# Two weight tiles at once in each output projection, and modulation vectors from one-column products

## The reference, cut to what matters

```python
mod = silu(c) @ ada_w[layer] + ada_b[layer]        # (3 * D,): shift, scale, gate
h = rms_norm(x, norm_w[layer]) * (1 + scale) + shift
y = mixer(h @ w_in)                                # layer's own mixer, its gate path with SiLU
x = x + gate * (y @ w_out)                         # w_out: 1024 x 1024
# after the last layer: out = rms_norm(x, final_norm_w)
```

## Time and profile before

| | us |
|---|---|
| median of 3 runs | 3574.63 |
| lowest, highest | 3570.79, 3578.21 |
| profiled execution, whole | 3582.37 |
| its span, first to last instruction | 3580.6 |
| TensorE busy in it | 3331.5 |

### The profile page before, as it was taken

One profiled execution on the slowest core, in us unless ns is written; L12 is line 12 of the kernel. 1 busy time (PEld: TensorE's weight loads), 2 busy tenths in 40 slices (PEclk: granted clock), 3 DMA queues, 4 the chain that ended last, 5 costly groups with the idle time before them and its releaser, 6 DMA issues.

```text
span 3580.6 us, 49279 instructions
## 1 busy us (share of the span) xinstructions
PE 3331.5 (93%) x18911; PEld 2689.9 (75%) x18911; DVE 2303.9 (64%) x3820; ACT 1509.9 (42%) x2635; POOL 943.0 (26%) x487
## 2 busy tenths in 40 slices
PE   5998899799999999999989999988998999999998
PEld 3776678677887777888767777876778777788877
DVE  6887888763466774565557766996536554556554
ACT  4665365333344124322466655653334431342234
POOL 1003233211233124222510043432121422422233
PEclk9999899899999999999989999998999999999999
DMA  4434455434753532111231123554449221221112
GB/s 170 131 111 129 126 145 147 124 105 127 251 179 89 166 93 88 50 37 36 65 129 55 46 72 84 159 139 111 126 112 349 74 59 53 60 72 40 32 48 100
DMA packets 569015, 383.83 MB, mean 107 GB/s; under 512 B 67802, under 2 KB 522445, under 8 KB 568781
## 3 DMA queue, kind: packets, MB, share of 16 engines
q1 hardware_dynamic: 568781, 380.68, 35.6%
HBM read 299.01 MB, written 80.54 MB: 106 GB/s over the span
## 4 chain that ended last, share of the span: by engine, by line
PE 71%; DVE 16%; DMA 4%; ACT 4%; issue 4%; SPq 1%; POOL 1%; ACTq 0%; DVEq 0%; POOLq 0%
PE bank L230 55%; DVE dnp_conv L1837 3%; DVE dnp_diag_term L1915 2%; DVE h_lo L700 1%; PE bank L2359 1%; DVE res_ada_sums L279 1%; DVE dnp_diag_inv L1918 1%; PE bank L2562 1%; DVE res_h L688 1%; DMA dn_planes<-dnp_inv_t 1%; PE bank L2589 1%; POOL w_lo L212 1%; PE bank L1527 1%; DVE res_sq_total L727 1%; PE bank L2603 1%
## 5 line engine op out<-in xcount | busy, mean ns | idle before, releaser
L230 PE MATMUL bank<-h_hi,w_hi 128*128 128x512 f32 x3616 | 1478.9, 409 | 49.6 <-DVE h_lo L126 16.0
L230 PE MATMUL bank<-h_hi,w_lo 128*128 128x512 f32 x3616 | 1428.0, 395 | 0.0
L230 PE MATMUL bank<-h_lo,w_hi 128*128 128x512 f32 x3616 | 1427.6, 395 | 0.0
L212 POOL TENSOR_TENSOR w_lo<-w_raw,w_hi 128x1024 fp32r<-128x1024 f32 x262 | 648.2, 2475 | 1447.8 <-ACT w_hi L203 1447.8
L230 PEld LDWEIGHTS bank<-h_hi,w_hi 128*128 128x128 f32 x3616 | 691.1, 191 | 227.4 <-issue 57.1
L230 PEld LDWEIGHTS bank<-h_lo,w_hi 128*128 128x128 f32 x3616 | 692.0, 191 | 148.6 <-issue 12.8
L230 PEld LDWEIGHTS bank<-h_hi,w_lo 128*128 128x128 f32 x3616 | 689.7, 191 | 150.8
L1837 DVE SCALAR_TENSOR_TENSOR dnp_conv<-dnp_raw,dn_conv_w,dnp_conv 128x512 f32<-128x512 f32 x288 | 267.1, 928 | 238.4 <-ACT dnp_conv L1659 231.1
L203 ACT ACTIVATE w_hi<-w_raw 128x1024 fp32r<-128x1024 f32 x292 | 306.1, 1048 | 71.5 <-DMA w_raw<-in_pool_w_in 24.8
L757 DVE SCALAR_TENSOR_TENSOR x_res<-bank,mod_gate,x_res 128x512 f32<-128x512 f32 x128 | 95.8, 749 | 268.6 <-PE bank L230 267.8
L844 ACT ACTIVATE res_sq<-x_res 128x512 f32<-128x512 f32 x160 | 101.0, 631 | 327.4 <-DVE x_res L757 225.4
(11 more groups left out here) (321 smaller groups left out, 4485.5 us busy)
## 6 DMA issues: line engine op xcount, KB each, us to landing
dnr_in<-dn_planes SPq DMA_DIRECT2D x112, 512.0 KB, 7.3
dn_planes<-y SPq DMA_DIRECT2D x192, 256.0 KB, 2.5
w_raw<-in_dn_w_in SPq DMA_DIRECT2D x64, 512.0 KB, 4.5
w_raw<-in_swa_w_in SPq DMA_DIRECT2D x36, 512.0 KB, 3.6
w_raw<-in_rg_w_in SPq DMA_DIRECT2D x32, 512.0 KB, 4.8
w_raw<-in_rg_w_out SPq DMA_DIRECT2D x32, 512.0 KB, 3.9
w_raw<-in_dn_w_out SPq DMA_DIRECT2D x32, 512.0 KB, 3.9
w_raw<-in_pool_w_in SPq DMA_DIRECT2D x32, 512.0 KB, 4.4
```

The lines of the kernel that those rows point to most:

```text
L212: alu.tensor_tensor(self.lo[j % SLOTS][:, :, :], self.raw[j % 2][:, :, :], self.hi[j % SLOTS][:, :, :].bitcast(F32), ALU.subtract).then_in ...
L230: ins = self.nc.tensor.matmul(out, w[slot][:, k, :], x[:, k, cols], start=(k == 0 and n == 0), stop=(k == KT - 1 and n == 2))
```

## The change

In short: (1) every output projection begins with `multiply_two`, which runs the first two tiles of d together, k by k, so that each split k feeds six matmuls; the ring of banks has three places, and weights are rounded and subtracted one tile earlier. (2) y of chunk 0 is split earlier: in the rg and swa phases around the last unit; the last `turn` and `weigh` of swa are put inside the two-tile product at k = 5 and k = 7. (3) In the first ingest and in the residual of layer 0, the modulation is made by TensorE alone, from one-column products of each piece by silu(c). (4) In the pool phase u of group 0, chunk 1, gets banks 6 and 7.

```diff
+    def multiply_two(self, pe, outs, j, x_hi, x_lo, cols, each_k, late=None):
+        for k in range(KT):
+            if late and k in late:
+                late[k]()
+            pe.wait_ge(*each_k[k])
+            for i, out in enumerate(outs):
+                slot = (j + i) % SLOTS
+                if k == 0:
+                    pe.wait_ge(self.split, j + i + 1)
+                for m, (w, x) in enumerate(((self.hi, x_hi), (self.hi, x_lo), (self.lo, x_hi))):
+                    ins = self.nc.tensor.matmul(out, w[slot][:, k, :], x[:, k, cols],
+                                                start=(k == 0 and m == 0), stop=(k == KT - 1 and m == 2))
+                if k == KT - 1:
+                    ins.then_inc(self.projected, 1)
...
+    def multiply(self, pe, first, last):
+        n = self.cols // P
+        for m in range(first, min(last, self.pieces)):
+            t, k = divmod(m, KT)
+            pe.wait_ge(self.loaded[m % self.bufs], 16 * (m // self.bufs) + 16)
+            for i in range(n):
+                ins = self.nc.tensor.matmul(self.bank[:, t * n + i:t * n + i + 1],
+                                            self.piece[m % self.bufs][:, i * P:i * P + P], self.core.cond[:, k:k + 1],
+                                            start=(m == 0 and i == 0), stop=(m == self.pieces - 1 and i == n - 1))
+            ins.then_inc(self.used, 1)
+            self.products = m + 1
...
-RING, SUMS = (0, 4), (5, 7)
+RING, SUMS = (4, 0, 1), (5, 7)
@@ residual_phase, SyncE @@
-                w.load_to(sp, tile0 + j + 3)
+                w.load_to(sp, min(tile0 + j + 4, after))
@@ residual_phase, TensorE @@
-                if j >= 2:
-                    pe.wait_ge(s_x, j - 1)
+                if j >= len(ring):
+                    pe.wait_ge(s_x, j - len(ring) + 1)
...
+                elif j == 0:
+                    two_tiles()
+                elif j > 1:
+                    w.multiply(pe, ring[j % len(ring)][:, :], tile0 + j, h_hi, h_lo, cs[c],
                                each_k=core.y_is_split(c) if d == 0 else None)
...
-                if late and j >= 6 and j % 2 == 0:
-                    late.reduce(pe, (j - 6) // 2)
+                if ada:
+                    ada.multiply(pe, j, j + 1)
+                if late and 3 <= j <= 14:
+                    late.multiply(pe, 4 * (j - 3), 4 * (j - 2))
@@ residual_phase, VectorE @@
-                if ada and c > 0:
-                    ada.accumulate(dve, d, d + 1)
-                if late and 3 <= j <= 14:
-                    late.accumulate(dve, 4 * (j - 3), 4 * (j - 2))
             if ada:
-                ada.accumulate(dve, KT, ada.pieces)
                 ada.finish(dve)
@@ residual_phase, ScalarE (GpSimd's subtract_to likewise), behind its fence @@
-                if not ingest and j:
-                    w.round_to(act, min(tile0 + j + 3, after))
+                if not ingest:
+                    w.round_to(act, min(tile0 + j + 4, tile0 + len(steps) + 2))
@@ rg_phase, ScalarE @@
+                if i == units - 1:
+                    core.round_y(act, 0, range(KT - 1))
                 copy(i)
...
-            core.round_y(act, 0, range(KT))
+            core.round_y(act, 0, [KT - 1])
+            w.round_to(act, w.tiles + 3)
             activate(units - 1)
-            w.round_to(act, w.tiles + 2)
@@ rg_phase, VectorE @@
+                if i == units - 1:
+                    core.lower_y(dve, V, 0, [0, 2])
                 convolve(i)
...
+                if i == units - 1:
+                    core.lower_y(dve, V, 0, [4, 6])
...
-            core.lower_y(dve, V, 0, range(0, KT, 2))
             combine(units - 1)
@@ pool_phase, TensorE @@
+            return bank[6 + t if g == 0 and c else t][:, :]
...
+                if n == 0:
+                    pe.wait_ge(s_u, NCH * GT)
                 pe.wait_ge(s_p, GT * n + GT)
...
-                if 2 * g + c:
+                if 2 * g + c > (0 if part else 1):
@@ swa_phase, GpSimd @@
+                if u == units - 1:
+                    core.lower_y(pool, nc.gpsimd, 0, range(2))
+                    w.subtract_to(pool, w.tiles + 2)
+                    core.lower_y(pool, nc.gpsimd, 0, range(2, KT - 2))
                 pool.wait_ge(s["rec"], u + 1)
@@ swa_phase, TensorE: last_turn and last_weigh hold what stood here @@
+            pe.wait_ge(s["logits"], 6 * units)
+            core.pe_tail = {KT - 3: last_turn, KT - 1: last_weigh}
@@ swa_phase, ScalarE @@
+                if u == units - 1:
+                    core.round_y(act, 0, range(KT - 1))
                 act.wait_ge(w.projected, q_product(u))
...
-            core.round_y(act, 0, range(KT - 1))
+            core.round_y(act, 0, [KT - 1])
+            w.round_to(act, w.tiles + 3)
             transposed(units, NCH - 1)
```

More of the change, by code:

```diff
@@ L53, in __init__ @@
         self.norms, self.mixers, self.sum_last = 0, 0, None
+        self.pe_tail = None
     def sb(self, name, shape, dt=F32, ctx=None):
@@ L252, in __init__ @@
         self.acc = [core.sb(f"{tag}_ada_sums{i}", [P, cols], F32, ctx) for i in range(accs)]
+        self.products = 0
         self.loaded = [core.sem(f"{tag}_ada_loaded{i}") for i in range(self.bufs)]
@@ L289, in reduce @@
         ins.then_inc(self.summed, 1)
+    def multiply(self, pe, first, last):
[9 more added lines that the diff above has]
+            self.products = m + 1
     def finish(self, dve):
-        dve.wait_ge(self.summed, len(self.blocks))
+        if self.products:
+            dve.wait_ge(self.used, self.pieces)
+        else:
+            dve.wait_ge(self.summed, len(self.blocks))
         core, V = self.core, self.nc.vector
@@ L633, in sum_squares, with two_tiles @@
                     .then_inc(s_sum, 1)
+            def two_tiles():
+                w.multiply_two(pe, [r[:, :] for r in ring[:2]], tile0, h_hi, h_lo, cs[0], core.y_is_split(0),
+                               core.pe_tail)
+                core.pe_tail = None
             def turn_x(j):
@@ L671, in _ @@
                 core.sum_last = lambda: sum_squares(NCH - 1)
[L672 to L676, removed]
             pe.wait_ge(s_x, len(steps) - 1)
@@ L885, in _ @@
             for j, (c, d) in enumerate(steps):
-                if not ingest and j:
-                    w.subtract_to(pool, min(tile0 + j + 3, after))
+                if not ingest:
+                    w.subtract_to(pool, min(tile0 + j + 4, tile0 + len(steps) + 2))
                 if not ingest and c + 1 < NCH and d % 2:
@@ L2363, in _ @@
             for i, (g, part, c, t) in enumerate(seq):
-                if 2 * g + c:
+                if 2 * g + c > (0 if part else 1):
                     pe.wait_ge(s_gate if part else s_u, GT * (2 * g + c - 1) + t + 1)
-                w.multiply(pe, bank[2 * part + t][:, :], tile0 + (2 * g + part) * GT + t, h_hi, h_lo,
+                w.multiply(pe, bank[GT + t][:, :] if part else u_bank(g, c, t), tile0 + (2 * g + part) * GT + t, h_hi, h_lo,
                            slice(c * CH, c * CH + CH), each_k=core.h_ready(c) if (g, part, t) == (0, 0, 0) else None)
@@ L2383, in _ @@
                 act.wait_ge(w.projected, product(g, part, c, t))
+                done = [j for j in range(tile0, w.tiles) if w.last[j] <= prod0 + i + 1]
+                if i < 2 + GT:
+                    w.round_to(act, tile0 + len(done) + 3)
                 if part == 0:
                     act.wait_ge(s_head, n + t + 1)
-                    nc.scalar.activation(u[t][:, HALO:HALO + CH], bank[t][:, :], ACT.Copy).then_inc(s_u, 1)
+                    nc.scalar.activation(u[t][:, HALO:HALO + CH], u_bank(g, c, t), ACT.Copy).then_inc(s_u, 1)
                 else:
@@ L2392, in _ @@
                     core.round_y(act, 0, range(KT))
-                done = [j for j in range(tile0, w.tiles) if w.last[j] <= prod0 + i + 1]
                 w.round_to(act, min(tile0 + len(done) + 3, w.tiles + 2))
@@ L2534, in _ @@
             sp.dma_start(kk[1][0:QW, QW:QW + HALF], kk[1][QW:P, QW:QW + HALF]).then_inc(s["keys_doubled"], 16)
-            w.load_to(sp, w.tiles + 2)
+            w.load_to(sp, w.tiles + 3)
             core.leave_sp(sp)
@@ L2547, in _ @@
                     .then_inc(s["probs"], 1)
-                w.subtract_to(pool, tile0 + 2 + u + 3)
-            core.lower_y(pool, nc.gpsimd, 0, range(1, KT - 1, 2))
+                w.subtract_to(pool, min(tile0 + 2 + u + 3, w.tiles + 2))
+            core.lower_y(pool, nc.gpsimd, 0, [KT - 2])
             core.leave(pool, "pool")
```

25 lines of the change are left out of this document (13 added, 12 removed).

## The result

| | before | after |
|---|---|---|
| median, us | 3574.62 | 3643.43 |
| runs, us | 3570.79 to 3578.21 | 3640.26 to 3648.18 |
| profiled execution, us | 3582.37 | 3640.26 |
| its span, us | 3580.6 | 3638.5 |
| TensorE busy in it, us | 3331.5 | 3429.1 |

The ratio of after to before is 1.0185, 95% interval 1.0172 to 1.0198: 66 us slower (69 by the two medians). The forecast was slower, 3595, and its range ended at 3613: the side was right, the size far off.

The account below looks back on a forecast made before the run. The prediction took TensorE, busy 93% of the span, to bound the kernel. Its terms, 27.4 + 6 + 8 - 4 - 8.5 - 6.5 - 2 = +20.4 us on the 3574.6 median, gave 3595 us; range 3554 to 3613.

Parts of the forecast that it names:

- First ingest: Half 0's ingest: one-column products on TensorE instead of VectorE's sums delay the vectors, +27.4 us.
- rival B: Narrow products count as work for the clock, so the ingest costs -4; 3556 us in all, chance 0.22.
- Second modulation: Layer 0's residual, half 0: 39 us of narrow products on TensorE replace 32.9 us lost to VectorE's lateness, +6 us.
- its clock: Layer 0's residual, half 0: several of 12 bursts end in a half-clock stretch, +8 us, bounds 0 and 20.
- Rival C: The clock falls for good, each burst followed by a cold product, handovers gain half; +42, 3617 us, chance 0.06.
- Handover rg to residual: From rg mixer to residual, both halves: a 5.3 us stall becomes 4.7 one product later; -2 each, -4 us.
- Handover swa to residual: From swa to residual, both halves: earlier start, partly lost to a 3.1 us stall at the transposes of x; -8.5 us.
- Pool's bank: Pool mixer's bank for u: half 1's 4.79 us wait goes, -6.5 us; in half 0 the gain turns idle, 0.
- Weights: Weights a tile earlier: five waits for `w_lo` go, -3.8 us, while chunk 1's rounding comes later; -2 us.
- The base: The profiled execution took 3582.4 us, 7.8 above the median; the predicted difference was put on the median, 3574.6.
- Slower: Whole kernel: slower by over 0.2% (7 us), chance 0.69.

Follow-up runs that it names:

- e12: Kernel before, with the transposes of x two products behind instead of one and nothing else; 3580.68 us, ratio 1.0011.
- e4b: Changed kernel, one-column products only in layer 0's residual, in rows of eight behind k = 3 and k = 7; 3583.79 us, ratio 1.0018.
- e10: Changed kernel without one-column products, x transposed two products behind, four banks in the ring of residuals that are not the last; 3547.19 us, ratio 0.9908.
- e7: Kernel before, with only the pool part of the change (banks, and earlier rounding of the next weight tile); 3570.88 us, ratio 0.9974.
- e2: Changed kernel with one-column products only in the ingest, the residual's vectors again sums on VectorE; 3595.96 us, ratio 1.0049.
- e1: Changed kernel without one-column products, both sets of modulation vectors made as before; 3568.02 us, ratio 0.9964.
- e3: Changed kernel with one-column products only in layer 0's residual, half 0, in 12 bursts of 16; 3610.69 us, ratio 1.0100.
- e4: As e3, but the 192 one-column products two behind each k of projections 4 to 15; 3631.14 us, ratio 1.0149.
- e5: As e4, but the one-column products start two projections later, at j = 6; median 3648.63 us, ratio 1.0110.

## Why the prediction was wrong, by its own steps

**First ingest, +27.4: right.** +28.4, and the price by which it came out, 0.43 us for a one-column product at half clock, held to the last piece. The Trainium skill (TensorE: Matmul & The Clock Gate, "LDWEIGHTS (loading the stationary operand)") would have had half of that; the records 0.215 us apart against 0.11 in the residual say that here the load went with the clock. One argument under rival B does not hold, though it took the right side: that transposes stayed at the slow pace in the first ingest was so in the kernel before and in e12, and not in ten other traces.

**Second modulation, +6, and its clock, +8: the failed step is the second.** The sum of the trace: 98.8 us for the residual without the modulation, 47.1 for the 384 records (start to start), 24.2 by which the twelve products behind the bursts exceed 5.45 us each, 1.2 of waits for pieces: 171.3, and 170.5 were measured. Of the 47.1, e4b, where the clock stood up, shows 41.0 as the price at full clock (predicted 39). It also shows 0.14 us more for a product each time it follows a row at full clock, 1.7 us for twelve. So the clock cost 24.2 - 1.7 + 6.1 = some 28 us, against 8 taken and 20 as the upper bound. The clock's own record agrees: the twelve stretches at 0.50 last 58 us together, and half of that is 29. The argument for the low end was that no burst is idle in full; TensorE was busy without a gap in eleven of the twelve, and the clock fell all the same. The bound was wrong too: it priced a cold stretch at 1.7 us, but four of them last 6.8 us or more, and five begin inside the burst, as the one at 375.5, so the one-column products pay too. Rival C had the twelve bursts at +20 with 0.06; its place was right.

**Handover rg to residual, -4: wrong, about 0.** The stall moved one product on as foreseen (4.84 us for the 4.7 predicted), but by x of product 0 and the ring, not by the weights of tile 4; these stand right behind it, as e10 shows. In half 1 the start gained 7.3 and lost the same.

**Handover swa to residual, -8.5: wrong, +0.9 and +1.7 in the two halves.** The early start is worth more than it said (7 to 10 us in each half for 4.1 and 5), the wait in return too: 5.4 us for 3.1, then half clock, and 0.9 at every second step after, which nothing in the prediction had. The 2.3 us between 3.1 and 5.4 are a term left out of the chain: VectorE splits the first tile of y of chunk 1 before it adds product 0 to x. VectorE in half 1 of the changed kernel:
```profile
3530.63 2.31 DVE L127 TENSOR_TENSOR h_lo<-y,h_hi 128x512 fp32r<-128x512 f32 x1 [2.15 <-ACT h_hi L118]
3532.86 1.40 DVE L795 SCALAR_TENSOR_TENSOR x_res<-bank,mod_gate,x_res 128x512 f32<-128x512 f32 x2
```
**Pool's bank, -6.5 and 0:** right within its error, 5 us by e7's trace and 5 to 13 by its times. **Weights, -2:** the waits in the residuals went (what is left, 4.8 us, is new and stands in the pool phase), chunk 1 gave back 0.5 to 0.7 in each residual; about -1 (read off the two traces, not tested alone).

**The base.** The working stood on a profiled execution 7.8 us above its median; that of after is 3.2 below its own. So 11 of the 48.8 us missed are between 57.9 (traces) and 68.8 (medians), and no step of the sum. The other 38 are, roughly, the clock (20), the handovers (some 14), and 4 for the pieces' full-clock price and waits.

**Chances.** Slower was right at 0.69, and not by luck: the ingest alone, +28 by the trace and +30 by e2, outweighs the 13 us that the rest gained by e1. Nearly every other term erred to the same side, and the range had let them cancel.

## What to carry to other kernels

Before work goes to TensorE, ask what it does to the clock, and not only how long it takes: here weight loads with one moved column behind each kept the engine busy, and it and the products behind them ran at half clock all the same. Whether they stood in rows of sixteen or of eight decided 27 to 29 us. Where two products alternate to hide a start, both end together, so what follows the first of them must be one product further away; here one constant gave back 15 us. The stall removed behind the recurrent mixer was found again one product later, where the ring waits for x, and with one bank more in the ring it was found at the weights.

## What was not expected of the hardware

- Each of twelve rows of 16 one-column products (3.5 us at full clock) brought 3.4 to 10.2 us at half clock, and twelve of twelve in e3 again; 24 rows of eight (1.7 us) brought none.
- The same instructions ran 88.8 us at 0.50 and then 64 us at 1.00, parted by 0.80 us of idle time and one sum of squares (e4). Another order of them gave 3594 us once and 3646 to 3655 three times (e5).
- 32 products of 512 moved fp32 columns over one stationary column took the first ingest to the fast pace from the second piece on and kept it there for 41 us; 128 products of one moved column never did in 67 us.
- Transposes alone took TensorE to 1.00 in the first ingest of ten traces and not in two; of the three traces with the ingest code of the kernel before, in one (e7).
